# Norm sums apart from the last block, inverted blocks requested ahead of the set, and a semaphore for the rows alone, in a one-core diffusion block

## The chip, the cores and the metric

The kernel runs on one core of one Trainium2 chip. The core has five engines that run their own instruction streams and meet through semaphores: TensorE (PE, matrix products), VectorE (DVE), ScalarE (ACT), GpSimd (POOL) and SyncE (SP, which here issues most of the DMAs). The metric is the device time of one execution in microseconds (us), lower is better; of several runs the median counts.

## The reference, cut to what matters

One layer of a diffusion backbone works on 256 latent tokens and 256 context tokens with 2048 channels each. A half-step SwiGLU feed-forward net (FFN1) runs over both streams, then a token mixer, then a second feed-forward net (FFN2) over the latent stream only, then a last norm. Each part begins with a root-mean-square norm and a shift and scale.

```
def rmsnorm(x, g):
    y = xf * lax.rsqrt(jnp.mean(xf * xf, axis=-1, keepdims=True) + EPS)
    return (y * g.astype(jnp.float32)).astype(x.dtype)
...
def chunk_gated_delta(q, k, v, g, beta, s0):
    """Chunked gated delta rule S_t = a_t S_{t-1}(I - b_t k_t k_t^T) + b_t k_t v_t^T, o_t = S_t^T q_t."""
    n = L // CHUNK
...
    sol = lax.linalg.triangular_solve(eye + a_low, rhs, left_side=True, lower=True, unit_diagonal=True)
    u_val, w_kd = sol[..., :GDN_DV], sol[..., GDN_DV:]
    qk = jnp.einsum('nbhid,nbhjd->nbhij', qc, kc) * decay

    def step(S, xs):
        q_i, k_i, u_i, w_i, g_i, qk_i = xs
        v_new = u_i - jnp.einsum('bhck,bhkv->bhcv', w_i, S)
...
def mixer_out(p, o, z, w_pool, pool_scale, o_norm_g, w_out):
    y = jnp.concatenate([pool_mixer(p[..., :POOL_W], w_pool, pool_scale),
                         gdn_gate_out(o, z, o_norm_g)], axis=-1)
    return y @ w_out
...
    for li in range(DEPTH):
        h = h + 0.5 * ml[:, 2][:, None] * swiglu(
            modulate(rmsnorm(h, norm_g[li, 0]), ml[:, 0], ml[:, 1]), ffn_w_in[li, 0], ffn_w_out[li, 0])
...
        pl = modulate(rmsnorm(h, norm_g[li, 1]), ml[:, 3], ml[:, 4]) @ w_in[li]
...
        h = h + ml[:, 5][:, None] * mixer_out(pl, ol_f + ol_b, zl, w_pool[li], pool_scale[li],
                                              o_norm_g[li], w_out[li])
        h = h + 0.5 * ml[:, 8][:, None] * swiglu(
            modulate(rmsnorm(h, norm_g[li, 2]), ml[:, 6], ml[:, 7]), ffn_w_in[li, 1], ffn_w_out[li, 1])
    return rmsnorm(h, final_g)
```

The DeltaNet part has 8 heads, chunks of 64 tokens and two directions; each chunk needs the inverse of a unit lower triangular 64 by 64 matrix.

## The kernel before, in words

Every weight is used as two parts: ACT writes the rounded high part `wh` of a tile that SP loaded into `raw`, DVE the rest `wl = raw - wh` (a *split*, about 1.2 us), and PE makes three products with them (L698, L699, L700). This pair of splits runs some tiles ahead of PE, in the order in which the tiles are used, and so also in every gap of the other work of ACT and DVE.

The stages in time: norm 0 and the modulation vectors (to 110 us), FFN1 (11 groups, to 1588), norm 1, the projections and preparation of the 8 heads (1601 to 1941), the token tiles of the pooling part (to 1977), eight scans (`scan(h)`, 1977 to 2156), the output projection, norm 2 (2203 to 2210), FFN2, norm 3 (2965) and the output.

**Norms.** ACT squares the 16 blocks of 128 channels of the residual as they are finished, into `sq[:, 0]` and `sq[:, 1]` in turn. POOL adds 14 of them into `nacc`. PE's `norm(n, ...)` then waits for all squares and sums over partitions with 128 by 1 products: for each tile of 128 tokens one of `nacc`, one of `sq[:, 0]`, one of `sq[:, 1]`, into one column of a bank (12 products for 512 tokens, 6 for 256). DVE's `mean_square` makes `n_ms`, POOL raises it to -0.5 (`n_rstd`), PE spreads it over the partitions, DVE and ACT make the normalized blocks `xh` and `xl` (`x2h` and `x2l` in norm 2), and PE starts on the next weights. In `normed`, DVE runs `between(m)`, a split of a coming weight tile, after each second block.

**The inversion.** `lanes(b, part)` on POOL inverts 32 by 32 diagonal blocks of four heads at a time (batch `b` = heads 4b to 4b+3) by 31 steps of two instructions each, in three parts (`LANE_STEPS`), and at the end copies `XL` transposed to `XP`. SP's `lane_store(b)` writes both to HBM (`d_x`, `d_xp`, 512 KB each, semaphore `fg_out`). For each head, `level_load(h)` reads eight 32 KB pieces back into `CX` and `CP` (after `placed` of the head before) and 384 KB of rows `UF` (after `pe_y64` of the head before), all on one semaphore, `level_in`. POOL's `place(h)` waits for these nine, copies the pieces into block diagonal places of `GI` and `FI` (16 copies, L2220 and L2226) and raises `placed`. PE's `join_y32(h)` and what follows (*the join* of head h, from L1075 on) wait for `placed` and build the inverse of the 64 by 64 matrices. `scan(h)` runs the join of head h+1 between its own first products; the join of head 0 runs inside the token tiles. `out_power(h)` on POOL serves the output norm of head h after its scan.

**SP's order.** SP works its requests in program order and waits in place. In the loop over the scans it first stores (`lane_store(1)`, in turn h = 2), then `set_load(h + 1)` (six requests, 1.7 MB, after `pe_av` of the head before last), then `level_load(h + 2)`, then tiles of the output weight (`out_load`). The calls `FILL_AT` place pieces of the pooling part (`pool_linear`, `means`) between the steps of a scan.

Of the kernel before, what the change touches and what calls it, by code (L numbers as in the profile page):

```python
# [13 lines left out]
P = 128  # L14
# [112 lines left out]
LANE_STEPS = (((0, 11), (11, 21), (21, BLK - 1)), ((0, 13), (13, 23), (23, BLK - 1)))  # L127
SET_DMAS = 6
LEVEL_DMAS = 2 * NBLK + 1
# [5 lines left out]
FILL_AT = ((3, 5, 6), (0, 1, 2, 3, 5, 6), (0, 1, 2, 3, 5, 6)) + 5 * ((0, 2, 3, 5, 6),)  # L135
# [78 lines left out]
def build(nc, xT, ctxT, cols_in, ada_in_w, masks_in, pools_in, w_out_t, w_ada, w_in, a_log, dt_bias,  # L214
# [14 lines left out]
    with es:  # L229
# [164 lines left out]
        mk_in, ba_in, rowc_in = sem("mk_in"), sem("ba_in"), sem("rowc_in")  # L394
# [57 lines left out]
        def bc(ap, n):  # L452

            return ap.unsqueeze(1).broadcast_to([P, n, ap.shape[-1]])

# [14 lines left out]
        def _(sp):  # L470
# [137 lines left out]
            def level_load(h):  # L608
# [26 lines left out]
            for h in range(HEADS + 2):  # L635
                for k in range(K_TILES):
# [25 lines left out]
            lane_load(HEADS - 1)  # L662
# [3 lines left out]
            level_load(1)  # L666
# [26 lines left out]
        def _(pe):  # L693
# [267 lines left out]
            def decay_sums():  # L961
                pe.wait_ge(prep_dve, PREP_G)
                pe.wait_ge(mk_in, 16)
# [94 lines left out]
            def join_y32(h):  # L1058

                sl, bank = h % 2, JOIN_BANK(h)  # L1060
                pe.wait_ge(HS["placed"], at("placed", h, 1))
                if h >= 2:
# [170 lines left out]
            norm(1, NTOK, 7)  # L1233
# [28 lines left out]
            norm(2, SEQ, 4)  # L1262
            with pe.Fori(0, GROUPS) as g:
                group(1, g, 0, T_FFN2, x_base=2 * KT)
            norm(3, SEQ, 4)
# [3 lines left out]
        def _(act):  # L1269
# [19 lines left out]
            def square(n, k, streams):  # L1289
# [3 lines left out]
                for s in range(streams):  # L1293
                    i = fn(sq[:, k % 2, s * SEQ:(s + 1) * SEQ], (h_lat, h_ctx)[s][:, k, :], ACT.Square)  # L1294
# [33 lines left out]
            def group(f, r, s, base, width=0, closing=None, early=None, begun=0):  # L1328
                for j in range(GROUP_TILES):
                    if j >= begun:  # L1330
# [16 lines left out]
            def squares(n, f, streams, blocks):  # L1347

                for k in blocks:
                    act.wait_ge(gated[f], gates(f, 0, LAST if f < 2 else 1, 0) + (k + 1) * streams)  # L1350
                    square(n, k, streams)

            def decay_prep():
                act.wait_ge(prep_dve, 1)
                act.wait_ge(rowc_in, 32)
# [206 lines left out]
            with act.Fori(0, PIECE_ONE) as r:  # L1562
# [3 lines left out]
                  early=decay_weights)  # L1566
            for k in range(K_TILES):
                high(1, 2 * k)
                high(1, 2 * k + 1)
                split(0, 0, T_HEADS + k + AHEAD)  # L1570
            act.wait_ge(x_ready, 2 * KT)
            act.dma_start(rowc[:, 0, :], dt_bias.rearrange("l d h -> l (d h)").broadcast_to([P, 16])).then_inc(rowc_in, 16)
            act.dma_start(rowc[:, 1, :], a_log.rearrange("l d h -> l (d h)").broadcast_to([P, 16])).then_inc(rowc_in, 16)
# [746 lines left out]
```

## Time and profile before

| | |
|---|---|
| runs | 2977.45, 2975.01, 2976.6 us; median 2976.6 us |
| profiled execution | 2981.67 us, its span 2979.8 us, mean granted clock of TensorE 0.982 |
| PE busy | 2885.3 us, 97% of the span |
| DVE / ACT / POOL busy | 1682.2 (56%) / 963.8 (32%) / 235.3 us (8%) |
| DMA | 541.62 MB, mean 182 GB/s |

The span is that of the profiled execution from the first to the last instruction; the time of that execution is 1.9 us longer. A busy time is the time in which the engine executes; PE is busy nearly throughout, so its idle stretches and the stretches in which its granted clock is low are what there is to look at.

### The profile page before, as it was taken

The numbers are of one execution on the slowest core, as the hardware profiler recorded it, in microseconds if no ns is written. First come the engines' busy times: TensorE is split into PE (matmuls) and PEld (weight loads), VectorE is DVE, ScalarE is ACT, GpSimd is POOL, SyncE is SP. The second block draws the span as 40 slices with busy tenths as digits, with TensorE's granted clock in tenths as the row PEclk, the third lists the DMA queues.
The fourth block names the chain that finished last, engine by engine and source line by source line (L and its number), as shares of the span: only waits on it lengthen the run. The fifth ranks groups of instructions, "written<-read, shape, count | busy, mean of one in ns | idle before, by whom it ended". The sixth has DMA issues, their size and how long they took to land. (4 is left out here: it accounts for less than half of the span.)

```text
span 2979.8 us, 47716 instructions
## 1 busy us (share of the span) xinstructions
PE 2885.3 (97%) x18176; PEld 2523.8 (85%) x18176; DVE 1682.2 (56%) x2465; ACT 963.8 (32%) x1434; POOL 235.3 (8%) x390
## 2 busy tenths in 40 slices
PE   5999999999999999999998999988989999999998
PEld 3677888888888888888887888868889999999998
DVE  2522557566575747566536666735565555555555
ACT  2212222222122222122124555533344443443443
POOL 3000000000000000000001113463120000000001
PEclk8999999999999999999999999989999999999999
DMA  9764255545455766757423566675555566565564
GB/s 361 285 211 159 92 155 156 164 147 169 140 174 171 247 198 224 230 192 259 142 85 88 152 191 189 197 226 153 158 155 181 185 186 187 181 187 183 183 190 133
DMA packets 399049, 541.62 MB, mean 182 GB/s; under 512 B 51024, under 2 KB 301904, under 8 KB 390240
## 3 DMA queue, kind: packets, MB, share of 16 engines
q1 hardware_dynamic: 377264, 434.20, 46.9%
q10 hardware_dynamic: 21680, 106.03, 11.0%
q8 instruction: 65, 1.06, 0.1%
q14 instruction: 40, 0.33, 0.0%
HBM read 518.08 MB, written 22.05 MB: 181 GB/s over the span
## 5 line engine op out<-in xcount | busy, mean ns | idle before, releaser
L1626 DVE TENSOR_TENSOR wl<-raw,wh 128x1024 fp32r<-128x1024 f32 x640 | 782.4, 1232 | 775.2 <-ACT wh L1278 773.5
L1278 ACT CAST wh<-raw 128x1024 fp32r<-128x1024 f32 x640 | 666.1, 1047 | 1548.1 <-PE ps L700 1177.4
L698 PE MATMUL ps<-xh,wh 128*128 128x512 f32 (+1 forms) x1920 | 733.7, 382 | 7.1 <-issue 4.6
L699 PE MATMUL ps<-xl,wh 128*128 128x512 f32 (+1 forms) x1920 | 724.3, 377 | 0.0
L700 PE MATMUL ps<-xh,wl 128*128 128x512 f32 (+1 forms) x1920 | 723.3, 377 | 0.0
L698 PE MATMUL ps<-hth,wh 128*128 128x512 f32 (+1 forms) x1408 | 471.3, 335 | 0.6 <-DVE wl L1626 0.6
L699 PE MATMUL ps<-htl,wh 128*128 128x512 f32 (+1 forms) x1408 | 470.3, 334 | 0.0
L700 PE MATMUL ps<-hth,wl 128*128 128x512 f32 (+1 forms) x1408 | 470.3, 334 | 0.0
L698 PEld LDWEIGHTS ps<-xh,wh 128*128 128x128 f32 x1920 | 363.5, 189 | 78.2 <-issue 9.4
L700 PEld LDWEIGHTS ps<-xh,wl 128*128 128x128 f32 x1920 | 362.8, 189 | 68.1
L699 PEld LDWEIGHTS ps<-xl,wh 128*128 128x128 f32 x1920 | 363.4, 189 | 64.7
L698 PE MATMUL ps<-x2h,wh 128*128 128x256 f32 x1408 | 395.6, 281 | 6.4 <-DVE x2l L1682 6.3
L699 PE MATMUL ps<-x2l,wh 128*128 128x256 f32 x1408 | 393.5, 279 | 0.0
L700 PE MATMUL ps<-x2h,wl 128*128 128x256 f32 x1408 | 393.4, 279 | 0.0
L1723 DVE SCALAR_TENSOR_TENSOR acc<-abuf,cT,acc 128x1024 f32<-128x1024 f32 x240 | 297.0, 1279 | 0.0
L698 PEld LDWEIGHTS ps<-hth,wh 128*128 128x128 f32 x1408 | 264.3, 188 | 29.2 <-DVE wl L1626 1.0
L700 PEld LDWEIGHTS ps<-hth,wl 128*128 128x128 f32 x1408 | 264.5, 188 | 27.5
L699 PEld LDWEIGHTS ps<-htl,wh 128*128 128x128 f32 x1408 | 263.8, 187 | 27.1
L698 PEld LDWEIGHTS ps<-x2h,wh 128*128 128x128 f32 x1408 | 265.0, 188 | 7.8 <-issue 7.7
L700 PEld LDWEIGHTS ps<-x2h,wl 128*128 128x128 f32 x1408 | 265.4, 188 | 0.0
L699 PEld LDWEIGHTS ps<-x2l,wh 128*128 128x128 f32 x1408 | 264.0, 188 | 0.0
L2183 POOL TENSOR_TENSOR nacc<-hf 128x512 f32<-128x512 f32 (+1 forms) x4 | 4.4, 1108 | 2250.7 <-ACT hf L1294 2250.7
(245 smaller groups left out, 2342.7 us busy)
## 6 DMA issues: line engine op xcount, KB each, us to landing
raw<-in_ffn_w_in SPq DMA_DIRECT2D x704, 256.0 KB, 3.2
raw<-in_ffn_w_out SPq DMA_DIRECT2D x176, 512.0 KB, 4.2
abuf<-in_w_ada ACTq DMA_DIRECT2D x64, 1024.0 KB, 6.0
ada_t<-in_ada SPq DMA_DIRECT2D x64, 512.0 KB, 9.1
abuf<-in_w_ada ACTq DMA_DIRECT2D x64, 512.0 KB, 3.7
raw<-in_w_in SPq DMA_DIRECT2D x128, 256.0 KB, 3.4
gate_t<-in_ada SPq DMA_DIRECT2D x32, 512.0 KB, 4.9
raw<-in_w_out SPq DMA_DIRECT2D x32, 512.0 KB, 4.3
```

Of the source, the lines that this page charges most:

```text
L698: mm(out, ah, bh, start=first, stop=False)
L699: mm(out, ah, bl, start=False, stop=False)
L700: return mm(out, al, bh, start=False, stop=last)
L1278: nc.scalar.copy(wh[:, t % HL, :], raw[:, t % RAW, :]).then_inc(hi_done, 1)
L1626: tt(wl[:, t % HL, :], raw[:, t % RAW, :], wh[:, t % HL, :].bitcast(F32), ALU.subtract).then_inc(lo_done, 1)
L1723: n = stt(acc[:, b, :], src, c_, acc[:, b, :], ALU.mult, ALU.add)
L2183: i = tt(nacc[:, 0:nt], sq[:, 0, 0:nt], sq[:, 1, 0:nt], ALU.add)
```

## The change

(a) `norm(n)`: PE sums `nacc` and `sq[:, 0]` as soon as 15 of the 16 blocks are squared, and the squares of the last block apart, into a bank of their own (`LAST_BANK`). DVE makes `n_ms` from the first sums and adds the last block's in a second instruction (`stt`); POOL waits for both. ACT's squares of a block wait for each stream apart.

(b) `normed`: in norm 1 one split is left out of the last FFN1 group (`left=1`) and done as the first `between`; in norm 2 the first `between` is empty; each of the others stands one place later and one at the end.

(c) SP: `level_load` becomes `level_blocks` (the eight pieces) and `level_rows` (`UF`, with a semaphore `rows_in` that PE's join waits for and POOL no longer). `lane_store(0)` is some tiles earlier, and so are the blocks and rows of head 0; `level_blocks(1)` is ahead of `set_load(0)`; in the loop over the scans `level_blocks(h + 2)` is ahead of `set_load(h + 1)`, except in turns 0 and 2; in turn 2 `set_load(3)` is ahead of `lane_store(1)`.

(d) POOL: `place(1)` follows `place(0)` at once; `lanes(1, part)` are one turn later against the places, and the second batch's parts are steps 0 to 12, 13 to 25 and 26 to 30 (before 13 to 22 and 23 to 30).

(e) The second scan has its fillers at other steps. (f) `mk_in` and `rowc_in` become one semaphore.

```diff
-LANE_STEPS = (((0, 11), (11, 21), (21, BLK - 1)), ((0, 13), (13, 23), (23, BLK - 1)))
+LANE_STEPS = (((0, 11), (11, 21), (21, BLK - 1)), ((0, 13), (13, 26), (26, BLK - 1)))
...
-FILL_AT = ((3, 5, 6), (0, 1, 2, 3, 5, 6), (0, 1, 2, 3, 5, 6)) + 5 * ((0, 2, 3, 5, 6),)
+FILL_AT = ((3, 5, 6), (0, 2, 3, 4, 5, 6), (0, 1, 2, 3, 5, 6)) + 5 * ((0, 2, 3, 5, 6),)
...
-            def level_load(h):
+            def level_blocks(h):
...
+            def level_rows(h):
+
                 if h:
                     sp.wait_ge(HS["pe_y64"], at("pe_y64", h - 1, 1))
                 sp.dma_start(UF[0:3 * BLK].rearrange("p m c -> p (m c)"),
-                             d_uf[h, 0:3 * BLK].rearrange("p m c -> p (m c)")).then_inc(HS["level_in"], 16)
+                             d_uf[h, 0:3 * BLK].rearrange("p m c -> p (m c)")).then_inc(rows_in, 16)
...
+                    if h == HEADS and k == K_TILES - 2:
+                        lane_store(0)
                     if h == HEADS + 1 and k == 0:
-                        lane_store(0)
+                        level_blocks(0)
+                        level_rows(0)
...
-                    if h == HEADS + 1 and k == 3:
-                        level_load(0)
...
+            level_blocks(1)
             lane_load(HEADS - 1)
             set_load(0)
             out_load(0)
             out_load(1)
-            level_load(1)
+            level_rows(1)
...
             for h in range(HEADS):
+
+                last = h in (0, 2)
+                if h + 2 < HEADS and not last:
+                    level_blocks(h + 2)
+                if h + 1 < HEADS:
+                    set_load(h + 1)
                 if h == 2:
                     lane_store(1)
-                if h + 1 < HEADS:
-                    set_load(h + 1)
                 if h + 2 < HEADS:
-                    level_load(h + 2)
+                    if last:
+                        level_blocks(h + 2)
+                    level_rows(h + 2)
...
             def norm(n, nt, bank):
 
+
                 pe.wait_ge(nacc_done, (KT - 3) * (n + 1))
-                pe.wait_ge(sq_done, KT * (n + 1))
+                pe.wait_ge(sq_done, KT * (n + 1) - 1)
                 for t in range(nt // P):
                     x_ = slice(t * P, (t + 1) * P)
                     mm(ps[:, bank, t:t + 1], nacc[:, x_], ones, start=True, stop=False)
-                    mm(ps[:, bank, t:t + 1], sq[:, 0, x_], ones, start=False, stop=False)
-                    i = mm(ps[:, bank, t:t + 1], sq[:, 1, x_], ones, start=False, stop=True)
+                    i = mm(ps[:, bank, t:t + 1], sq[:, 0, x_], ones, start=False, stop=True)
+                i.then_inc(stat_pe, 1)
+                pe.wait_ge(sq_done, KT * (n + 1))
+                for t in range(nt // P):
+                    i = mm(ps[:, LAST_BANK[n], t:t + 1], sq[:, 1, t * P:(t + 1) * P], ones, start=True, stop=True)
                 i.then_inc(stat_pe, 1)
...
             def squares(n, f, streams, blocks):
 
+                last = gates(f, 0, LAST if f < 2 else 1, 0)
                 for k in blocks:
-                    act.wait_ge(gated[f], gates(f, 0, LAST if f < 2 else 1, 0) + (k + 1) * streams)
-                    square(n, k, streams)
+                    square(n, k, streams, lambda s: act.wait_ge(gated[f], last + k * streams + s + 1))
...
+                dve.wait_ge(stat_pe, 2 * n + 2)
+                stt(m, ps[:, LAST_BANK[n], 0:nt // P], 1.0 / D, m, ALU.mult, ALU.add).then_inc(ms_done, 1)
...
                 low(n, KT - 1)
                 between(KT // 2 - 1)
+                between(KT // 2)
...
-            normed(2, SEQ, 4, lambda k: split(0, 0, T_FFN2 + k + AHEAD))
+            normed(2, SEQ, 5, lambda m: split(0, 0, T_FFN2 + m + AHEAD - 1) if m else None)
...
             place(0)
+            place(1)
             lanes(1, 0)
-            for h in range(HEADS):
+            for h in range(1, HEADS):
                 if h + 1 < HEADS:
                     place(h + 1)
-                if h:
-                    out_power(h - 1)
-                if h + 1 < len(LANE_STEPS[1]):
-                    lanes(1, h + 1)
+                out_power(h - 1)
+                if h < len(LANE_STEPS[1]):
+                    lanes(1, h)
             out_power(HEADS - 1)
```

How the instructions stand at three places of two engines:

POOL before, from the last copy of `place(0)` on: the zeroing of `XL` and then 13 inversion steps of the second batch, the last of which is the sixth row, ahead of the first copy of `place(1)`.

```order
L2226 COPY FI<-CX 32x4x32
L2240 MEMSET XL 128x1024 [waits fg_out,lt_in,gdn_placed]
L2242 MEMSET XL 128x32 [waits xl_zero]
L2249 TENSOR_TENSOR tm<-LT,XL 128x31 [waits xl_zero]
...
L2254 TENSOR_TENSOR XL<-XL,tm 128x19x13 [waits lane_step]
L2220 COPY GI<-CX 32x4x32 [waits gdn_pe_tn64,gdn_level_in,lane_step]
```

POOL of the change at the same place:

```order
L2255 COPY FI<-CX 32x4x32
L2249 COPY GI<-CX 32x4x32 [waits gdn_pe_tn64,gdn_level_in,gdn_placed]
...
L2255 COPY FI<-CX 32x4x32
L2269 MEMSET XL 128x1024 [waits fg_out,lt_in,gdn_placed]
L2271 MEMSET XL 128x32 [waits xl_zero]
L2278 TENSOR_TENSOR tm<-LT,XL 128x31 [waits xl_zero]
```

`place(1)` has moved ahead of the first part of the inversion of the second batch.

POOL before, from the last copy of `place(2)` to `place(3)`: `out_power(0)`, then the third part of the second batch to its end and `XP`.

```order
L2226 COPY FI<-CX 32x4x32
L2192 TENSOR_TENSOR ors<-oms,mhalf 128x2 [waits gdn_oms_set,gdn_placed]
L2249 TENSOR_TENSOR tm<-LT,XL 128x192 [waits lane_step,gdn_ors_set]
...
L2254 TENSOR_TENSOR XL<-XL,tm 128x31 [waits lane_step]
L2257 COPY XP<-XL 128x1024 [waits lane_step]
L2220 COPY GI<-CX 32x4x32 [waits gdn_pe_tn64,gdn_level_in,lanes_done]
```

POOL of the change, from the end of the second part to `place(4)`: `place(3)` and `out_power(1)` now stand ahead of the third part.

```order
L2283 TENSOR_TENSOR XL<-XL,tm 128x6x26 [waits lane_step]
L2249 COPY GI<-CX 32x4x32 [waits gdn_pe_tn64,gdn_level_in,lane_step]
...
L2255 COPY FI<-CX 32x4x32
L2221 TENSOR_TENSOR ors<-oms,mhalf 128x2 [waits gdn_oms_set,gdn_placed]
L2278 TENSOR_TENSOR tm<-LT,XL 128x135 [waits lane_step,gdn_ors_set]
L2283 TENSOR_TENSOR XL<-XL,tm 128x5x27 [waits lane_step]
...
L2286 COPY XP<-XL 128x1024 [waits lane_step]
L2249 COPY GI<-CX 32x4x32 [waits gdn_pe_tn64,gdn_level_in,lanes_done]
```

The end of the inversion of heads 4 to 7 has moved behind the output norm of the second scan.

SP before, in turn 2 of the loop over the scans: the store of the second batch (`d_x`, `d_xp`), then the set of head 3 (`s_khT` to `s_z`), then the pieces of head 4.

```order
L633 DMA raw<-in_w_out 128x1024 [waits lo_done]
L590 DMA d_x<-XL 128x1024 [waits lanes_done]
L590 DMA d_xp<-XP 128x1024
L604 DMA s_khT<-d_khT 128x512 [waits gdn_pe_av,gdn_y_set]
...
L606 DMA s_z<-d_z 128x256
L616 DMA CX<-d_x 32x8x32 [waits gdn_placed,fg_out]
```

SP of the change in the same turn:

```order
L639 DMA raw<-in_w_out 128x1024 [waits lo_done]
L607 DMA s_khT<-d_khT 128x512 [waits gdn_pe_av,gdn_y_set]
...
L609 DMA s_z<-d_z 128x256
L593 DMA d_x<-XL 128x1024 [waits lanes_done]
L593 DMA d_xp<-XP 128x1024
L619 DMA CX<-d_x 32x8x32 [waits gdn_placed,fg_out]
```

The store stands right ahead of the reading of what it stored, behind the set.

## Rows read from the trace of the kernel before

**Rows 1.** What PE waits for: releaser, us in all, count, longest.

```profile
PE ps L1075 <- POOL FI L2226: 18.7, 6, 8.6
PE ps L732 <- POOL n_rstd L2189: 11.2, 4, 7.8
PE ps L698 <- DVE x2l L1682: 6.3, 4, 2.7
PE ps L1211 <- DVE yl L2069: 3.8, 2, 2.0
```

**Rows 2.** Timeline at norm 1: start, us, engine, line, operation [idle before <- releaser].

```profile
1589.30 0.40 ACT L1294 ACTIVATE hf<-h_ctx 128x256 f32<-128x256 f32 x1
1589.85 0.35 PE L726 MATMUL ps<-cols,nacc 128*128 128x1 f32 x2 [1.81 <-ACT hf L1294]
1593.08 0.16 DVE L1660 TENSOR_SCALAR n_ms<-ps 128x4 f32<-128x4 f32 x1 [1.18 <-PE ps L728]
1594.40 2.07 PE L732 MATMUL ps<-cols,n_rstd 128*128 128x128 f32 x8 [1.35 <-POOL n_rstd L2189]
```

**Rows 3.** Windows by stage: stretch, us; PE, PEld, DVE, ACT, POOL busy; PEclk; DMA; GB/s.

```profile
1954.00:1977.00 23.00, 22.56 (x183) 17.80 (x184) 7.40 (x9) 7.79 (x13) 11.63 (x21) 0.85 0.95 302
1977.00:2009.80 32.80, 22.40 (x207) 19.69 (x207) 8.64 (x26) 9.35 (x29) 27.66 (x62) 0.74 0.57 189
2009.80:2038.00 28.20, 23.94 (x227) 20.93 (x226) 12.50 (x37) 9.36 (x27) 13.14 (x34) 0.88 0.30 85
2038.00:2057.60 19.60, 19.00 (x245) 18.04 (x244) 13.08 (x37) 8.77 (x26) 3.53 (x9) 1.00 0.89 257
2057.60:2077.60 20.00, 17.61 (x233) 16.58 (x232) 11.59 (x34) 8.29 (x28) 4.81 (x18) 1.00 0.63 196
2077.60:2141.50 63.90, 58.60 (x692) 55.41 (x691) 37.51 (x102) 23.54 (x69) 13.77 (x45) 0.89 0.53 160
```

**Rows 4.** PE's timeline where the joins of heads 0, 1 and 4 begin.

```profile
1954.44 0.37 PE L1075 MATMUL ps<-GI,UF 32*32 32x32 f32 x6 [3.89 <-POOL FI L2226]
...
1988.73 0.26 PE L1075 MATMUL ps<-GI,UF 32*32 32x32 f32 x2 [8.63 <-POOL FI L2226]
...
2060.16 0.22 PE L1075 MATMUL ps<-GI,UF 32*32 32x32 f32 x2 [1.96 <-POOL FI L2226]
```

**Rows 5.** POOL's timeline from the token tiles to the scan of head 2.

```profile
1949.01 0.28 POOL L2220 COPY GI<-CX 32x128 f32<-32x128 f32 x1 [14.85 <-DMA UF<-d_uf]
...
1951.83 1.19 POOL L2226 COPY FI<-CP 32x128 f32<-32x128 f32 x1
...
1984.20 0.28 POOL L2220 COPY GI<-CX 32x128 f32<-32x128 f32 x1
...
2013.91 0.41 POOL L2249 TENSOR_TENSOR tm<-LT,XL 128x135 f32<-128x135 f32 x1
...
2018.08 1.98 POOL L2257 COPY XP<-XL 128x1024 f32<-128x1024 f32 x1
...
2039.33 0.69 POOL L2192 TENSOR_TENSOR ors<-oms,mhalf 128x2 f32<-128x2 f32 x1 [2.60 <-DVE oms L1969]
...
2054.64 0.28 POOL L2220 COPY GI<-CX 32x128 f32<-32x128 f32 x1 [14.61 <-DMA UF<-d_uf]
```

**Rows 6.** DVE's timeline: a split in the token tiles, and one in norm 2.

```profile
1951.60 1.26 DVE L1626 TENSOR_TENSOR wl<-raw,wh 128x1024 fp32r<-128x1024 f32 x1 [3.19 <-ACT wh L1278]
...
2215.82 1.23 DVE L1626 TENSOR_TENSOR wl<-raw,wh 128x1024 fp32r<-128x1024 f32 x1 [3.07 <-ACT wh L1278]
```

**Rows 7.** SP's queue in the scan of head 2: issue start, us, line, transfer.

```profile
2042.38 0.32 SPq L604 DMA_DIRECT2D s_khT<-d_khT  x1
...
2045.63 0.45 SPq L606 DMA_DIRECT2D s_z<-d_z  x1
```

**Rows 8.** DMA issues of 2037 to 2056 and 1986 to 2000: KB each, median us to landing.

```profile
d_xp<-XP SPq DMA_DIRECT2D x1, 512.0 KB, 6.0
...
CX<-d_x SPq DMA_DIRECT2D x4, 32.0 KB, 2.0
```

More of the change, by code:

```diff
@@ L393, in build @@
             sem("fin_done"), sem("fin_pool"), sem("fin_scaled"), sem("rb_set"), sem("out_done"))
-        mk_in, ba_in, rowc_in = sem("mk_in"), sem("ba_in"), sem("rowc_in")
+        ba_in, prep_in, rows_in = sem("ba_in"), sem("prep_in"), sem("rows_in")
         ba_hi, ba_split, ba_done, prep_dve, prep_act, prep_pe = (
@@ L962, in decay_sums @@
                 pe.wait_ge(prep_dve, PREP_G)
-                pe.wait_ge(mk_in, 16)
+                pe.wait_ge(prep_in, 48)
                 for q in range(4):
@@ L1061, in join_y32 @@
                 pe.wait_ge(HS["placed"], at("placed", h, 1))
+                pe.wait_ge(rows_in, 16 * (h + 1))
                 if h >= 2:
@@ L1232, in _ @@
                 group(0, r, 3, 3 * GROUP_TILES, reduced=True)
-            norm(1, NTOK, 7)
+            norm(1, NTOK, 6)
             pe.wait_ge(ba_split, 1)
@@ L1261, in _ @@
                 out_heads(d, range(HEADS))
-            norm(2, SEQ, 4)
+            norm(2, SEQ, 5)
             with pe.Fori(0, GROUPS) as g:
                 group(1, g, 0, T_FFN2, x_base=2 * KT)
-            norm(3, SEQ, 4)
+            norm(3, SEQ, 5)
         @block.scalar
@@ L1287, in start, with square @@
                 fn(cT[:], cols[:, C_C:C_C + 2 * KT], ACT.Silu).then_inc(c_silu, 1)
-            def square(n, k, streams):
+            def square(n, k, streams, final=None):
                 if k >= 2:
@@ L1293, in square @@
                 for s in range(streams):
+                    if final is not None:
+                        final(s)
                     i = fn(sq[:, k % 2, s * SEQ:(s + 1) * SEQ], (h_lat, h_ctx)[s][:, k, :], ACT.Square)
@@ L1565, in _ @@
             group(0, 0, LAST, LAST * GROUP_TILES, closing=lambda b: squares(1, 0, 2, range(4 * b, 4 * b + 4)),
-                  early=decay_weights)
+                  early=decay_weights, left=1)
             for k in range(K_TILES):
@@ L1569, in _ @@
                 high(1, 2 * k + 1)
-                split(0, 0, T_HEADS + k + AHEAD)
+                split(0, 0, T_HEADS + k + AHEAD - 1)
+            split(0, 0, T_HEADS + K_TILES + AHEAD - 1)
             act.wait_ge(x_ready, 2 * KT)
-            act.dma_start(rowc[:, 0, :], dt_bias.rearrange("l d h -> l (d h)").broadcast_to([P, 16])).then_inc(rowc_in, 16)
-            act.dma_start(rowc[:, 1, :], a_log.rearrange("l d h -> l (d h)").broadcast_to([P, 16])).then_inc(rowc_in, 16)
-            act.dma_start(mk[:], masks_in.rearrange("p (m n) -> p m n", n=P)).then_inc(mk_in, 16)
+            act.dma_start(rowc[:, 0, :], dt_bias.rearrange("l d h -> l (d h)").broadcast_to([P, 16])).then_inc(prep_in, 16)
+            act.dma_start(rowc[:, 1, :], a_log.rearrange("l d h -> l (d h)").broadcast_to([P, 16])).then_inc(prep_in, 16)
+            act.dma_start(mk[:], masks_in.rearrange("p (m n) -> p m n", n=P)).then_inc(prep_in, 16)
             for h in range(HEADS):
@@ L1605, in _ @@
                 high(2, 2 * k + 1)
-                split(0, 0, T_FFN2 + k + AHEAD)
+                if k:
+                    split(0, 0, T_FFN2 + k + AHEAD - 1)
+            split(0, 0, T_FFN2 + K_TILES + AHEAD - 1)
             group(1, 0, 0, T_FFN2, begun=K_TILES)
@@ L1658, in mean_square @@
             def mean_square(n, nt, bank):
[L1659 to L1660 removed]
+                m = n_ms[:, 0:nt // P]
+                dve.wait_ge(stat_pe, 2 * n + 1)
+                ts(m, ps[:, bank, 0:nt // P], 1.0 / D, EPS, ALU.mult, ALU.add).then_inc(ms_done, 1)
+                dve.wait_ge(ms_done, 2 * n + 1)
+                dve.wait_ge(stat_pe, 2 * n + 2)
+                stt(m, ps[:, LAST_BANK[n], 0:nt // P], 1.0 / D, m, ALU.mult, ALU.add).then_inc(ms_done, 1)
             SCALE = ((0, 1), (2, 3), (4,))
@@ L1771, in decay_weights, with group @@
                 tt(wbal[:], wba[:], wbah[:].bitcast(F32), ALU.subtract).then_inc(ba_split, 1)
-            def group(f, r, s, base, evac=False, width=0, then=None, late=None, begun=0):
+            def group(f, r, s, base, evac=False, width=0, then=None, late=None, begun=0, left=0):
                 for j in range(GROUP_TILES):
-                    if j >= begun:
+                    if begun <= j < GROUP_TILES - left:
                         split(r, GROUP_TILES, base + j + AHEAD)
@@ L1804, in decay_prep @@
                 dve.wait_ge(ba_done, 2)
-                dve.wait_ge(rowc_in, 32)
+                dve.wait_ge(prep_in, 48)
                 link(tt(xg, ba[:, :, 16:32], bc(rowc[:, 0, :], 4), ALU.add))
@@ L2131, in _ @@
                 group(0, r, 7, 7 * GROUP_TILES, evac=True, width=2)
-            group(0, 0, LAST, LAST * GROUP_TILES, evac=True, then=modulations, late=decay_weights)
-            normed(1, NTOK, 7, lambda k: split(0, 0, T_HEADS + k + AHEAD))
+            group(0, 0, LAST, LAST * GROUP_TILES, evac=True, then=modulations, late=decay_weights, left=1)
+            normed(1, NTOK, 6, lambda m: split(0, 0, T_HEADS + m + AHEAD - 1))
             dve.wait_ge(x_ready, 2 * KT)
```

17 lines of the change are left out of this document (8 added, 9 removed).

## Prediction

> **What bounds the kernel now.** I read the page first: PE is busy for 97% of the span, and the chain that ended last is nearly all PE. A change that doesn't touch PE's products can therefore win only PE's idle time, and the time that a low clock adds to its work. So the second view is what PE waits for [rows 1]. The join of a head waited for POOL's copies six times, 18.7 us in all; the norms waited 11.2 us for `n_rstd` (7.8 of it in norm 0), 6.3 us for DVE's low parts in norm 2, and 3.8 us twice for the pooling part `yl`. These four lines are 40 us, and the change aims at all four. The third view is the windows by stage [rows 3], for the granted clock: the scan of head 0, which holds the longest wait, has 0.74; that of head 2, where no join waits, and that of head 3, with one wait of 1.96, have 1.00; the three after them, 0.89 together. A low clock here means 1.2 instead of 2.4 GHz for part of the stretch. An unstalled scan is read from the row of 2057.60: 20.00 us less its wait of 1.96 [rows 4] leaves 18.04 us at clock 1.00.
>
> The profiled execution took 2981.67 us, 5.1 us above the median of the runs, 2976.6. I sum the terms against the former and carry the difference over to the median.
>
> **The norms.** In norm 1 the last square ends at 1589.70 [rows 2], PE starts its 12 sums at 1589.85, and DVE has `n_ms` at 1593.08: 3.4 us for twelve sums. With the change eight of them run before the last square is there and four stay behind it. Two thirds of the 3.2 us from the first sum to `n_ms` are 2.1; I take 2.0. ACT's squares no longer wait for both streams, which I put at one square's 0.4, so **2.4** (2.0 to 2.8). The new second instruction of DVE replaces one of 0.16 us on the path, so it costs nothing there; the first one is done early, hidden by the last square. In norms 2 and 3 six sums become two behind the last square, half of norm 1's: **0.9** each. In norm 0 there is one DVE instruction more and DVE is the late engine: **-0.2**. In norm 2 a split on DVE waited 3.07 us for ACT's high part [rows 6], and the low parts of the blocks queued behind it; PE waited for them four times, 6.3 us, the longest (2.7) for the first block, which stays. The other three, 3.6 us, go if the split stands one place later: by then PE has used the tile whose place ACT's high part waits for, and two more blocks' low parts stand ahead of it in DVE's queue. So norm 2 is 0.9 + 3.6 = **4.5** (0.9 to 4.5).
>
> **Token tiles and the join of head 0.** PE waited 3.89 us [rows 4]. `place(0)` started at 1949.01, released by the rows `UF` [rows 5], which the copies don't use. With `rows_in` apart and the requests earlier in SP's queue it can start earlier; I take 2.5 us, since the pieces themselves still cost eight requests and their landing, and `place(0)` also waits for the last spills of `q` and `z`. The stage has a clock of 0.85 over 23.00 us [rows 3], which is 3.45 us missing. I take 2.9 of it back, so **5.4**; ends: 2.5 (the wait alone) and 7.3 (3.89 + 3.45).
>
> One copy in `place(0)`, 1951.83, took 1.19 us where its like take 0.28, while DVE's split of 1951.60 to 1952.86 ran [rows 5, 6]. The Trainium skill (SBUF — State Buffer, "Who interferes with whom") says that a DVE instruction with two SBUF inputs contends with a GpSimd instruction that reads SBUF, and the split is one; the row agrees. It speaks against part (d): the last inversion steps move from a stretch of POOL without splits into the scan of head 2, where DVE splits. By the rule that part would cost one such excess, 0.9, more, and the sum would be 30.7 instead of the 31.6 below; I go by the measured duration without it.
>
> **Scan of head 0.** `place(1)` started at 1984.20 [rows 5], only after 13 inversion steps, and PE waited 8.63 for it [rows 4]. With the change it stands right behind `place(0)`, waits only for the join of head 0 to release `GI`, and takes some 4.5 us (1984.20 to 1988.73): it is done near 1969, and PE wants it near 1975 to 1980. The wait goes: 8.6. The clock missing in this scan is 0.26 x 32.80 = 8.5 us; none of it on work would give 8.6, two fifths of it 12.0. I take the middle, **10.3**. The first part of the second batch now runs behind `place(1)`, under the first scan, where nothing waits for it.
>
> **Scan of head 1.** 28.20 us at clock 0.88 [rows 3], with the two waits for `yl` of 3.8 us in all [rows 1] and 0.12 x 28.20 = 3.4 us of missing clock, 7.2 together. The new places of the fillers give DVE one step more between `pool_linear` parts; I expect one of the two waits to go (1.8), the other to shorten to 1.5, and most of the clock to come back: **5.0** (2.0 to 7.2).
>
> **Scan of head 2** has no wait and full clock, so **0**.
>
> **Scan of head 3: the price.** This is where the stall goes. In the kernel before, the second batch was inverted by 2020.06 (`XP` 2018.08 + 1.98), long before the scan of head 2 began at 2038.0. Now its last five steps and `XP` stand behind `out_power(1)`, which ended at 2040.0 (2039.33 + 0.69) [rows 5]. These steps and the copy took 2013.91 to 2020.06 = 6.15 us, so they end 8.2 us into that scan, at 2046.2 in the old times. The store stands behind the set of head 3, which SP issued from 2042.38 to 2046.1 [rows 7], so the queue costs nothing more: set and inversion end together. Store: 0.9 us to issue two, and 6.0 to land [rows 8], gives 2053. Then eight requests at 0.45 us each and 2.0 to land [rows 8], 5.7, gives 2058.8, and `place(4)`, 5.5 us in this place (2054.64 to 2060.16) [rows 4, 5], 2064.3. PE wanted it at 2058.2 (2060.16 less 1.96). Queueing in the DMAs moves this by a us or so either way; I take a stall of 5.5 where 1.96 was, -3.5. The last three scans lose 1.9 us of clock each with waits of 1 to 2 us (below); for this longer one I take 2.5: **-6.0** together. Ends: -11 if the store waits a further 5 us, and +2 if the chain is done in time.
>
> **Scans of heads 4 to 6.** 63.90 us [rows 3]; three unstalled ones are 3 x 18.04 = 54.1, so 9.8 can be won. Their three waits for POOL are 18.7 - 3.89 - 8.63 - 1.96 = 4.2 us [rows 1, 4]; the rest, 5.6, is clock, 1.9 a scan. `place` now starts on the pieces alone: `place(4)` of before was released by `UF` [rows 5], as were these. Since `level_blocks` stand ahead of the set, they are requested as soon as the previous head is placed, and the copies end before PE comes: **9.3**, from 4.2 (clock not regained) to 9.8.
>
> **Edits at nothing.** The merged semaphore `prep_in`: three transfers that land long before their use. The earlier `lane_store(0)` and pieces of head 0: they push the weight tiles behind them in SP's queue by ten requests of 0.45 us, 4.5 us, covered by the tiles that are loaded ahead; without that cover PE would lose up to those 4.5 us once. `set_load(h + 1)`, now behind eight requests of 0.45 us (3.6 us) that wait for `placed(h + 1)`: it waited for `pe_av` some 4.4 us into the scan anyway (2042.38 against 2038.0), and lands well before the next scan wants it.
>
> **Sum.** -0.2 + 2.4 + 5.4 + 10.3 + 5.0 + 0 - 6.0 + 9.3 + 4.5 + 0.9 = 31.6. The profiled execution would be at 2950.1, the median at 2976.6 - 31.6 = 2945. All low ends together give 9.9 (2967), all high ones 46.7 (2930).
>
> **The rivals.** *B, no new wait at head 4*: the store lands faster than 6.0 and the pieces are read in under 5.7 us, so that the -6.0 becomes 0 to +2: 2938. For it: the queue is less loaded than when the row was taken. Against: four dependent steps in series, each from a row. *C, only the waits go*: the clock doesn't come back since other short waits remain on PE, or POOL, whose order is now two places and then inversion, is late in the scan of head 1. Then the terms are 2.5 + 8.6 + 2.0 + 4.2 for the scans, -6 for head 4, 5.9 for the norms less part of norm 2: about 17, 2960. For it: three waits of 4.2 us together went with 5.6 us of missing clock. *D, nothing moves*: the waits are replaced by others of the same length, as when the pieces arrive late because all eight stand ahead of sets and rows: 2976. Against: the 8.63 are in POOL's order alone, and that is changed. *E, slower*: `set_load(h + 1)` is stuck behind `level_blocks(h + 2)`, which waits for `placed(h + 1)` while SP stands. If the place of the next head is done only 12 us or more after a scan's start, the set lands too late and the next scan begins late; the excess would be some 9 us in each of the four scans where this order applies, 37 us, against the 31.6 won: 2982. It decides from placing about 11 us into the scan; the row of before has 2.5 us (2060.1 against 2057.6) and the new order aims lower.
>
> **Chances.** My sum 0.55, B 0.15, C 0.22, D 0.04, E 0.04. Runs of this kernel can't tell changes under about 0.2%, 6 us, from none. Faster by more: 0.92; within: 0.04; slower: 0.04. The range goes from 2932 (most of B) to 2964 (most of C); D and E and the tails of the others stay out. The predicted time is that of my sum, 2945.
>
> **What would show it.** In the changed profile the wait of PE at the first product of the join should be under 2 us for head 0, gone for heads 1, 2, 3, 5, 6 and 7, and 4 to 7 us for head 4, with the store of the second batch issued some 8 us into the scan of head 2. PE's clock should be near 1.00 in the scans of heads 0, 1, 4, 5 and 6 and lower in that of head 3. Between the last square and `n_ms` of norm 1 there should be about 1.4 us, and in norm 2 one wait for a low part where four were. I am wrong if the clock stays low without long waits (C), if the chain of the second batch is shorter than its four steps (B), or if a set lands after its scan wants it (E).

## The result and the profile after

The changed kernel took 2953.82 us (median of 7 runs, 2928.54 to 2957.31) where before took 2977.85 (7 runs, 2975.01 to 2980.98): the ratio is 0.9921, 95% interval 0.9891 to 0.995. That is 24.0 us faster; 31.6 had been forecast, and the time lies inside the range of 2932 to 2964. One of the seven executions of the change came some 25 us earlier than the rest, as did four of twelve of x10 below and three of 19 of before in the comparison of x9 and x10; gains here are differences of medians, from which the ratios of x9 and x10 therefore stand apart, and nothing here shows why some come early.

The profiled execution of the change took 2957.31 us with a span of 2955.5 (before 2979.8). What PE waited for, to be read beside [rows 1]:

```profile
PE ps L750 <- POOL n_rstd L2218: 9.0, 4, 5.3
PE ps L1094 <- POOL FI L2255: 6.2, 2, 5.1
PE ps L1200 <- ACT vn L1522: 3.8, 1, 3.8
PE ps L712 <- DVE x2l L1710: 2.7, 1, 2.7
PE ps L1063 <- DVE AY L1954: 2.3, 1, 2.3
PE ps L1230 <- ACT u L1558: 1.6, 1, 1.6
```

The six waits for POOL's copies are two, and of 18.7 us 6.2 are left. The waits for `x2l` went from four to one, and the two waits for `yl` of the pooling part became one for `u` at the same product. Two lines are new: 3.8 us for `vn` (the new values of a scan's step, `v_new` in the reference, which ACT copies out of PE's banks), and 2.3 us for `AY` (a matrix that DVE makes in the preparation of a head). The windows of the same stages as in [rows 3] (token tiles, then the scans of heads 0, 1, 2, 3 and 4 to 6; the columns are those of rows 3):

```profile
1948.00:1971.20 23.20, 22.91 (x197) 17.86 (x195) 7.95 (x10) 8.21 (x14) 10.14 (x30) 1.00 0.97 287
1971.20:1998.70 27.50, 23.19 (x204) 20.36 (x205) 10.33 (x28) 9.93 (x30) 17.43 (x38) 0.75 0.77 253
1998.70:2021.10 22.40, 20.42 (x227) 18.45 (x227) 12.58 (x37) 9.39 (x27) 20.09 (x38) 1.00 0.34 105
2021.10:2043.10 22.00, 20.54 (x244) 19.51 (x243) 13.49 (x36) 8.81 (x25) 8.63 (x18) 0.92 0.51 160
2043.10:2069.00 25.90, 20.54 (x232) 19.43 (x232) 11.67 (x34) 8.25 (x28) 9.13 (x33) 0.80 0.68 211
2069.00:2122.90 53.90, 52.66 (x692) 49.75 (x691) 36.94 (x102) 23.60 (x69) 11.51 (x35) 1.00 0.63 190
```

The last row is the plainest: three scans in 53.90 us at clock 1.00, 17.97 each, where 63.90 at 0.89 stood. The row above it is the price: the scan of head 3 takes 25.90 at 0.80, where it took 20.00 at 1.00. The scan of head 0 got shorter, but its clock (0.75) hasn't recovered.

At norm 1, ACT, DVE and PE of the change, to be read beside [rows 2]:

```profile
1588.95 0.42 ACT L1315 ACTIVATE hf<-h_ctx 128x256 f32<-128x256 f32 x1
...
1590.69 0.16 DVE L1688 SCALAR_TENSOR_TENSOR n_ms<-ps,n_ms 128x4 f32<-128x4 f32 x1 [0.81 <-PE ps L746]
...
1592.01 2.08 PE L750 MATMUL ps<-cols,n_rstd 128*128 128x128 f32 x8 [1.43 <-POOL n_rstd L2218]
```

From the end of the last square to `n_ms` are 1.3 us (1589.37 to 1590.69) where 3.4 were; 1.4 had been forecast.

For the balance I took the starts and ends of the same PE instructions in both traces (the scans from the first product of `vn` and `s_kd`, a part of the head's set, in one to that in the next) and set the differences beside the terms of the prediction. us gained:

| stage | forecast | measured |
|---|---|---|
| norm 0, modulation, FFN1 | -0.2 | 0.0 (1523.21 to 1523.18) |
| norm 1, last product of FFN1 to first of the heads | 2.4 | 2.4 (13.01 to 10.65) |
| heads' projections up to the join of head 0 | 0 | -2.7 (349.50 to 352.17) |
| token tiles and the join of head 0 | 5.4 | 6.1 (3.89 to 0, 22.85 to 20.71) |
| scan of head 0, with its start | 10.3 | 5.2 (2.10 to 4.48, 30.41 to 22.80) |
| scan of head 1 | 5.0 | 5.8 (28.23 to 22.38) |
| scan of head 2 | 0 | -2.4 (19.57 to 22.02) |
| scan of head 3 | -6.0 | -5.9 (19.99 to 25.89) |
| scans of heads 4 to 6 | 9.3 | 10.0 (63.92 to 53.91) |
| norm 2 and the blocks behind it | 4.5 | 5.0 (7.43 to 6.53, 754.16 to 750.07) |
| norm 3 | 0.9 | 0.8 (4.84 to 4.05) |
| sum | 31.6 | 24.3 |

One pair of executions doesn't resolve every row of this table. Up to the end of FFN1 all the kernels below run what the change runs; in their profiles FFN1 ended between 1584.5 and 1588.3 us, and norm 1 took 9.7 to 10.7. In the scans of heads 2 and 3, x10 has the same instructions in the same order as the change:

```profile
2018.78:2039.26 20.48, 19.04 (x245) 18.01 (x243) 14.44 (x36) 8.84 (x26) 8.48 (x18) 1.00 0.52 167
2039.26:2067.15 27.89, 20.54 (x232) 19.43 (x231) 11.68 (x34) 8.26 (x28) 9.12 (x33) 0.82 0.65 200
```

There the two took 20.48 and 27.89 us, in the change 22.02 and 25.89: nearly the same together, 1.5 and 2.0 us apart by themselves, with waits of 1.01 and 7.13 us where the change has 1.04 and 5.14.

### The profile page after: what moved, and what is told of

Its sections match the earlier page's. It is cut to its first block and busy times, and to the rows that moved or that the text cites. A ratio compares the mean times of both kernels' runs of the same rounds, so it can differ in the third digit from the quotient of the medians.

```text
span 2955.5 us, 47731 instructions
## 1 busy us (share of the span) xinstructions
PE 2880.7 (97%) x18176; PEld 2521.3 (85%) x18176; DVE 1683.2 (57%) x2469; ACT 963.9 (33%) x1434; POOL 235.9 (8%) x390
```

## The experiments

Unless said otherwise each kernel is the change with one edit. All were timed beside the kernel before, whose medians were 2977.4 to 2978.9 us; the gains below are against those. Executions of one kernel commonly lie 3 to 12 us apart, so where a time differs from the change's by less than some 6 us, the profile has to tell the two apart.

**The end of the second batch** (x3; the term of -6.0). The edit:

```diff
-LANE_STEPS = (((0, 11), (11, 21), (21, BLK - 1)), ((0, 13), (13, 26), (26, BLK - 1)))
+LANE_STEPS = (((0, 11), (11, 21), (21, BLK - 1)), ((0, 18), (18, BLK - 1)))
...
+                if h == 2:
+                    lane_store(1)
                 if h + 1 < HEADS:
                     set_load(h + 1)
-                if h == 2:
-                    lane_store(1)
```

> The change, but the second batch is inverted in two parts, steps 0 to 17 and 18 to 30 with the copy XP, so that it ends ahead of the copies of head 3, and SP stores it ahead of the set of head 3. Theory (the wait of 5.14 us at head 4 and the half clock behind it are the price of the late end of the batch): store about 10 us earlier, no wait at head 4, the scan of head 3 at 18 instead of 25.9 us: 7.9 us faster than the change, about 2946. Rival (18 steps are too long for POOL ahead of the copies of head 2, and the wait only moves to heads 2 and 3): waits of 3 us or more there, 2952 to 2956.

Measured: 2945.32 us, ratio 0.9885 (0.987 to 0.99), a gain of 33.6, which is 9.5 beyond the change. First the chain in the profile of the change, from POOL's, SP's and PE's timelines; these are the links of the forecast:

```profile
2028.69 2.06 POOL L2286 COPY XP<-XL 128x1024 f32<-128x1024 f32 x1
...
2044.33 0.28 POOL L2249 COPY GI<-CX 32x128 f32<-32x128 f32 x1 [13.59 <-DMA CP<-d_xp]
```

```profile
2029.10 0.43 SPq L609 DMA_DIRECT2D s_z<-d_z  x1
2030.77 0.32 SPq L593 DMA_DIRECT2D d_x<-XL  x1
2031.13 0.43 SPq L593 DMA_DIRECT2D d_xp<-XP  x1
2038.48 0.32 SPq L619 DMA_DIRECT2D CX<-d_x  x1
```

```profile
2048.90 0.32 PE L1094 MATMUL ps<-GI,UF 32*32 32x32 f32 x4 [5.14 <-POOL FI L2255]
```

The inversion ends at 2030.75 (9.6 us into the scan; 8.2 forecast), SP stores at once, reads back 7.7 us later when the store has landed, POOL copies from 2044.33, and PE waits 5.14 us. In the experiment the same links, from POOL and SP:

```profile
2013.30 1.97 POOL L2286 COPY XP<-XL 128x1024 f32<-128x1024 f32 x1
2015.33 0.28 POOL L2249 COPY GI<-CX 32x128 f32<-32x128 f32 x1
...
2035.11 0.28 POOL L2249 COPY GI<-CX 32x128 f32<-32x128 f32 x1 [12.76 <-DMA CP<-d_xp]
```

```profile
2020.53 0.43 SPq L593 DMA_DIRECT2D d_x<-XL  x1
...
2028.51 0.38 SPq L619 DMA_DIRECT2D CX<-d_x  x1
```

`XP` is there 15 us earlier, the store is issued 10 us earlier, and the copies 9. PE's list of waits has no row for `FI` above 0.9 us; the scans of heads 2 and 3 take 19.59 and 17.97 where the change has 22.02 and 25.89. The theory holds: the wait at head 4 was the late end of the batch. The wait at head 3 (1.04 us in the change) went too: steps 18 to 30 took 14.6 us, steps 13 to 25 in the change 17.9, so that even with `XP` (2.0) ahead of it `place(3)` starts at 2015.33, in the change at 2017.21. The rival's waits at heads 2 and 3 didn't come.

**POOL's order at head 1** (x2; the wait of 8.6). `lanes(1, 0)` and `place(1)` change places:

```diff
             place(0)
-            place(1)
             lanes(1, 0)
+            place(1)
```

> The change, but POOL does the first part of the second batch's inversion ahead of the copies of head 1, as before. Theory (the 8.6 us wait of head 1 came from POOL's order alone): the inversion part runs about 1961 to 1979, the copies end near 1983.5, PE waits some 6.5 us for them and loses 2 us of clock: 8.5 us slower than the change, about 2962. Rival (requesting the pieces ahead of the set did it): no wait at head 1, 2954.

Measured: 2964.67 us, ratio 0.9953 (0.994 to 0.9967); 14.2 us won, 9.8 less than by the change. On PE:

```profile
1980.45 0.27 PE L1094 MATMUL ps<-GI,UF 32*32 32x32 f32 x2 [9.38 <-POOL FI L2255]
```

The wait is back, 3 us longer than I had worked out, in spite of the pieces requested early. POOL's order made it.

**The new wait for `vn`** (x6; the forecast did not have it). In the change, ACT at the start of the first scan:

```profile
1973.58 1.04 ACT L1297 CAST wh<-raw 128x1024 fp32r<-128x1024 f32 x1 [1.75 <-DMA raw<-in_w_out]
1974.65 1.07 ACT L1615 COPY u<-ps 128x512 f32<-128x512 f32 x2
1975.61 0.45 ACT L1522 COPY vn<-ps 128x128 f32<-128x128 f32 x2
```

`vn` stands in ACT's queue behind the high part of the third tile of the output weight, and that waited for the tile to land. PE came there 5.7 us earlier than before (1972.18 instead of 1977.89), the tile landed only 3.4 us earlier (1973.56 instead of 1977.00), since the set, two tiles and `UF` are ahead of it. The edit puts it ahead:

```diff
             lane_load(HEADS - 1)
-            set_load(0)
             out_load(0)
             out_load(1)
-            level_rows(1)
             out_load(2)
+            set_load(0)
+            level_rows(1)
             out_load(3)
```

> The change, but SP requests the first three tiles of the output weight ahead of the set of head 0. Theory (the new wait of 3.77 us for ACT's vn at the start of the first scan comes from the third of these tiles, whose landing ACT's queue waits for ahead of vn): it lands 5 us sooner, the wait falls to about 1.5 us as before, and the half clock of the 13 us after it mostly goes: 4 us faster, about 2950. Rival (vn waits for its own chain): wait unchanged, 2954; or the set lands too late and PE waits for it, 2956.

Measured: 2947.20 us, ratio 0.9903 (0.9888 to 0.9918), 6.8 us beyond the change. The first two scans in windows:

```profile
1966.50:1987.10 20.60, 18.46 (x204) 16.14 (x205) 7.28 (x25) 7.59 (x27) 16.04 (x40) 1.00 0.95 300
1987.10:2011.20 24.10, 22.12 (x228) 19.71 (x228) 12.81 (x37) 9.38 (x27) 21.70 (x43) 0.93 0.36 107
```

The wait is gone (a new one of 0.84 us for the set, which lands later, stands ahead of that scan), the first scan has clock 1.00 instead of 0.75 and takes 20.60 instead of 27.50. Measured between the same products, its start went from 4.48 to 0.81 us and its length from 22.80 to 19.74: the wait of 3.8 us had cost 6.7 with the low clock (1.2 GHz in part of the stretch) that went with it. The next three scans together give 0.6 of it back. That of head 1 takes 24.05 (22.38) at clock 0.93, with no wait for POOL; why its clock fell isn't shown. That of head 2 takes 19.60 (22.02) without the wait for POOL. That of head 3 takes 27.23 (25.89): POOL's inversion doesn't get faster, PE comes to the join of head 4 earlier and waits 7.48 us for it.

**The semaphore or the order, heads 5 to 7.** One kernel (x4) keeps the order and makes `place` wait for the rows again; the other (x5) keeps the semaphore and puts the pieces behind the set:

```diff
                 pool.wait_ge(HS["level_in"], at("level_in", h, PER["level_in"]))
+                pool.wait_ge(rows_in, 16 * (h + 1))
```

> The change, but POOL's copies of each head also wait for the rows, as before (SP's order stays the new one). Theory as the prediction put it (the copies of heads 5 to 7 win because they start on the pieces alone): their waits of 1 to 2 us and the lost clock are back, 9 us, with some more at heads 1 and 4: about 2966 to 2970. Rival (the order of the requests alone frees heads 5 to 7, since the copies wait for the scan's vn products anyway, 2 us behind the pieces): no wait at heads 5 to 7; only heads 1 to 4 shift, because the rows of head 1 land 10 us behind its pieces and hold back the inversion: waits at heads 2, 3 and 4 grow by 1, 3 and 5 us, about 2963.

```diff
-                last = h in (0, 2)
+                last = True
```

> The change, but SP requests the pieces of head h + 2 behind the set of head h + 1 in every turn of the loop over the scans, as before; the copies still don't wait for the rows. Theory (heads 5 to 7 need one of the two, the order or the semaphore, not both: behind the set the pieces land about 13.3 us into a scan, the copies end at 17.8, and PE comes at 18.6): no wait at heads 5 to 7, 2954 as the change. Rival (the prediction's reason: they win because the pieces stand ahead of the set): waits of 1 to 2 us and lost clock in three scans, about 2960 to 2963.

Measured: 2965.00 (0.9952, 0.9939 to 0.9966) and 2959.22 (0.9942, 0.9929 to 0.9956). PE's waits for POOL in the first, with the rows of heads 4 and 6 and POOL's start of `place(4)`, then those of heads 6 and 7 in the second:

```profile
PE ps L1094 <- POOL FI L2256: 15.8, 7, 9.3
...
2051.96 0.26 PE L1094 MATMUL ps<-GI,UF 32*32 32x32 f32 x2 [9.31 <-POOL FI L2256]
...
2092.78 0.22 PE L1094 MATMUL ps<-GI,UF 32*32 32x32 f32 x2 [2.71 <-POOL FI L2256]
...
2047.43 0.28 POOL L2250 COPY GI<-CX 32x128 f32<-32x128 f32 x1 [16.39 <-DMA UF<-d_uf]
```

```profile
2081.06 0.22 PE L1094 MATMUL ps<-GI,UF 32*32 32x32 f32 x2 [1.36 <-POOL FI L2255]
2100.13 0.25 PE L1094 MATMUL ps<-GI,UF 32*32 32x32 f32 x4 [1.03 <-POOL FI L2255]
```

Neither theory holds whole. The scans of heads 4 to 6 took 58.9 us with the order alone (18.20, 22.25, 18.40) and 56.6 with the semaphore alone (18.17, 19.39, 19.07); with neither 63.9, with both 53.9. In time either part wins half or more, and their gains overlap (5.0 and 7.3, together 10.0). In waits it is otherwise: of 4.2 us with neither, 3.2 are left with the order alone and 2.5 with the semaphore alone, and only both together remove them. Most of what one part wins alone is clock: five of these six scans have 1.00, that with the wait of 2.71 us 0.92, where before had 0.85, 0.92 and 0.92. By time alone x5 can't be told from the change; its profile is of its fastest execution (2951.73).

About half of what it costs to wait for the rows is elsewhere, but not for the reason that the rival gave. At head 1 a wait of 1.43 us came back (the scan of head 0 takes 24.95 instead of 22.80), and the wait at head 4 grew from 5.14 to 9.31. `place(1)` does start only when the rows have landed (1971.04 instead of 1962.69), but POOL waits for DVE at `out_power(0)` in both kernels and has made up for it there (1998.96, in the change 1998.47): `XP` is done 9.5 us into the scan of head 2, in the change 9.6, and the waits at heads 2 and 3 didn't grow. What is late is `place(4)` itself: its pieces had landed at 2045.00, its rows only at 2047.23, and that is 2.2 us of the 4.2; another 1.6 come from PE, which is there earlier because the scan of head 2 took 20.45 us and not 22.02.

**The norms alone** (x1). The kernel before with parts (a), (b) and (f); SP's and POOL's orders and the fillers of before.

> Only parts (a), (b) and (f) of the change; SP's and POOL's orders, the parts of the inversion and the fillers are those of before, and the copies of a place wait for the rows too, as before. Theory (the norm terms of the prediction are each a gain of their own): 2.4 + 4.5 + 0.9 - 0.2 = 7.6 us, so about 2970 where before has 2977.8; first product of norm 1 some 2.4 us earlier, in norm 2 one wait for a low part instead of four. Rival (what norm 1 wins is waited for again in the heads' projections, where the profile of the change shows a wait of 2.25 us for AY that before had not): 5 us, about 2973, with that wait in this profile too.

Measured: 2969.15 us, ratio 0.9969 (0.9957 to 0.998), 9.7 us won (the interval, 6 to 13 us, holds the 7.6 of the theory and the rival's 5 lies just outside). In the profile norm 1 takes 10.64 us, norm 2 6.53 and the blocks behind it 749.54, as in the change. The wait for `AY` is in it too, so it can't come from SP's or POOL's order:

```profile
PE ps L1059 <- DVE AY L1950: 1.8, 1, 1.8
```

It is not the norms' either: five of the other kernels (x2, x4, x5, x6 and x7) have the same instructions up to there and no such wait, and their heads take 349.5 to 349.8 us.

**The split of norm 2 at its old place** (x10), in ACT's program and in DVE's:

```diff
-                if k:
-                    split(0, 0, T_FFN2 + k + AHEAD - 1)
-            split(0, 0, T_FFN2 + K_TILES + AHEAD - 1)
+                split(0, 0, T_FFN2 + k + AHEAD)
...
-            normed(2, SEQ, 5, lambda m: split(0, 0, T_FFN2 + m + AHEAD - 1) if m else None)
+            normed(2, SEQ, 5, lambda m: split(0, 0, T_FFN2 + m + AHEAD) if m < K_TILES else None)
```

> The change, but in norm 2 the splits stand at the places of before. Theory (three of the four waits of norm 2 come from the split that stands one place too early in DVE's queue): the waits of 1.40, 1.11 and 1.10 us are back, 3.6 us slower, about 2957. Rival (the norm's apart sums removed them, since all of it is earlier by 0.9 us): one wait only, 2954.

Measured: 2956.47 us, ratio 0.9918 (0.9882 to 0.9953), which alone doesn't tell it from the change. The profile does:

```profile
PE ps L712 <- DVE x2l L1708: 6.3, 4, 2.7
```

The four waits are those of [rows 1], and the blocks behind norm 2 take 755.12 us where the change has 750.07. The split's place made them; the apart sums didn't remove them.

**The fillers of the second scan as before** (x8):

```diff
-FILL_AT = ((3, 5, 6), (0, 2, 3, 4, 5, 6), (0, 1, 2, 3, 5, 6)) + 5 * ((0, 2, 3, 5, 6),)
+FILL_AT = ((3, 5, 6), (0, 1, 2, 3, 5, 6), (0, 1, 2, 3, 5, 6)) + 5 * ((0, 2, 3, 5, 6),)
```

> The change, but the fillers of the second scan at the steps of before. Theory (the fillers were worth one of the two waits for the pooling part): two waits of 2.0 and 1.8 us where the change has one of 1.55, and half clock behind them: 3 to 5 us slower, 2957 to 2959. Rival (that scan is faster for the clock alone, because the first scan no longer ends late): one wait, 2954.

Measured: 2958.85 us, ratio 0.9933 (0.992 to 0.9947), 4.9 less won than by the change; here too the profile has to tell:

```profile
PE ps L1230 <- DVE yl L2098: 3.8, 2, 2.0
PE ps L1094 <- POOL FI L2255: 8.5, 2, 7.0
```

Both waits for `yl` are back and that scan takes 26.57 us instead of 22.38; the next takes 19.72 instead of 22.02, since POOL then has the time for its 13 steps ahead of `place(3)`, and the one after 27.71. The filler's places are worth 4.2 us in their scan, some of it passed on.

**Both remedies together** (x7), the earlier end of the batch (18 and 13 steps) and the tiles ahead of the set:

> The change with the second batch ended sooner and the first three output tiles ahead of the set of head 0. Theory (the two are independent): the gains of both add, 8.5 and 4 us, about 2941. Rival (the first scan's wait only moves the same work): 2945.

Measured: 2946.75 us, ratio 0.9902 (0.9887 to 0.9917). They don't add: 31.2 us won, 7.2 beyond the change, where 9.5 and 6.8 would be 16.3. With the first scan shorter, 18 steps are too many ahead of `place(2)`:

```profile
1993.35 0.24 PE L1094 MATMUL ps<-GI,UF 32*32 32x32 f32 x3 [3.44 <-POOL FI L2255]
```

The scan of head 1 takes 30.69 us. **Cut otherwise** (x9), into 15 and 16 steps:

```diff
-LANE_STEPS = (((0, 11), (11, 21), (21, BLK - 1)), ((0, 18), (18, BLK - 1)))
+LANE_STEPS = (((0, 11), (11, 21), (21, BLK - 1)), ((0, 15), (15, BLK - 1)))
```

> The change with the first three output tiles ahead of the set of head 0, and the second batch in two parts of 15 and 16 steps (before its store ahead of the set of head 3). Theory (with the first scan shorter, POOL's inversion sets the pace; 18 steps ahead of the copies of head 2 were too long by 3.4 us, and 13 left POOL idle for 2.4 us, room for two steps): no wait above 2 us at heads 2, 3 and 4, scans of 20, 23, 20.5 and 18 us, about 2939 where the two edits with 18 steps gave 2947. Rival (POOL has too much to do for the shorter scans whichever way it is cut): a wait of 3 us or more at head 3 or 4, 2945.

Measured: 2945.06 us, ratio 0.9907 (0.9875 to 0.9939). The wait at head 2 is gone, the one at head 3 is 3.21 us (scans of 20.12, 24.01, 23.80 and 17.95):

```profile
PE ps L1094 <- POOL FI L2255: 4.6, 2, 3.2
```

That is the rival's case. POOL has the same work in a shorter time, and with the tiles ahead of the set one join waited in each of the three cuts that were run: head 4 with 13, 13 and 5 steps (7.48 us, x6), head 2 with 18 and 13 (3.44, x7), head 3 with 15 and 16 (3.21, x9). The kernels x3, x9, x7 and x6 are 33.6, 32.4, 31.2 and 30.8 us under before; their intervals overlap, so which of them is fastest isn't shown.

## Why the prediction was right, point by point

- **The direction and the larger part of the sum** came as forecast: 24.0 of 31.6 us, about half way between the sum and the 17 of rival C. Of the waits that the change aims at the long ones of heads 0 and 1, three of four in norm 2 and those of heads 5 to 7 are gone, and the clock came back in the token tiles and in the scans of heads 1 and 4 to 6 (1.00). There rival C (only the waits go) is wrong; in the scan of head 0 (0.75) what it said came true, and the sign that the prediction named for that scan failed. B fell by the wait of 5.14 us at head 4; D and E fell by the time.
- **The price at head 4** was forecast by four links in series as a wait of 5.5 us and -6.0; measured 5.14 and -5.9, and shown by moving its cause (x3). That the numbers meet so closely is luck in part. Against the forecast the inversion ended 1.4 us later in the scan, the store took 0.8 longer and `place(4)` 0.9 less; and PE came 2.4 us later, since the scan of head 2 had become that much longer, which the forecast didn't have. In x10, where that scan took 20.48 us, the same chain made a wait of 7.13, and the scan of head 3 lost 7.9 where 6.0 had been forecast.
- **One of these links is a size**: the steps and `XP` took 2023.57 to 2030.75, 7.2 us instead of 6.15. One step took 1.10 us beside a split on DVE, 0.24 before without one:

```profile
2027.19 1.10 POOL L2278 TENSOR_TENSOR tm<-LT,XL 128x31 f32<-128x31 f32 x1
...
2026.91 1.29 DVE L1650 TENSOR_TENSOR wl<-raw,wh 128x1024 fp32r<-128x1024 f32 x1 [0.54 <-ACT wh L1297]
```

The rule that the prediction set beside the row (the Trainium skill, SBUF — State Buffer, "Who interferes with whom") would have put it 0.9 higher, and that is nearly the 1.0 measured. I went by the row without splits; for this link the rule would have been nearer. But the 5.5 us that the prediction took for `place(4)` had such a meeting in them too, and the 4.6 us of the change had none, so that over both links the two cancel. From the trace of before:

```profile
2055.43 1.28 POOL L2220 COPY GI<-CP 32x128 f32<-32x128 f32 x1
...
2055.29 1.27 DVE L1626 TENSOR_TENSOR wl<-raw,wh 128x1024 fp32r<-128x1024 f32 x1 [2.25 <-ACT wh L1278]
```

- **The scan of head 0 is the term that was mis-sized**: 10.3 forecast, 5.2 measured. The 8.6 us of POOL's order went, as forecast (x2). But the prediction asked only for what the join waits. PE came earlier to `vn` by more than the weight tile in ACT's queue ahead of it, so a wait of 1.5 us there grew to 3.8, and the scan kept a clock of 0.75. x6, which asks for that tile and the two before it ahead of the set, gave 6.8 us back.
- **The scan of head 2** was forecast at 0 and lost 2.4: ten steps of the inversion ahead of `place(3)` became thirteen, and I had moved the parts in the sum without their size. That made the wait of 1.04 us at head 3, where the prediction's own sign was none; it is gone in x3 and x8, with scans of 19.59 and 19.72. The rest is clock (0.92) and is not tied to that wait: x4, x5 and x10 have the wait (0.99 to 1.02), a clock of 1.00 and scans of 20.45 to 20.49.
- **The heads' projections** lost 2.7 us in this profile with a wait for `AY`. The change doesn't touch that stage; other profiles with the same instructions there have it or don't. What decides it stays open, and it is no part of the change.
- **Heads 5 to 7**: the size was right (9.3; 10.0), the reason half right. The prediction put it to the pieces alone and to their order; in time either half wins half or more alone, but only both together remove the waits (x4, x5).
- **The norms**: 2.4, 0.9 and 0.8 where 2.4, 0.9 and 0.9 were forecast; the split's place (3.6 forecast, 4.1 in the balance) is shown by x10.
- **Two slips in the prediction's sums** change little: eight requests of 0.45 us and 2.0 to land make 5.6 us, not 5.7, and all high ends together give 46.3, not 46.7, which is still 2930.

## What to carry to other kernels

When an engine is freed from one wait, look through each queue that it meets next for what doesn't come earlier by as much: here a weight tile that lands only 3.4 us earlier took half of the gain of its scan, and the wait for it cost 1.8 times its length, since the clock fell with it. When work of an off-path engine is moved behind something, follow it through every later step up to the one that waits (inversion, store, read, copy, join); here such a sum from single rows came out within half a microsecond, but only because links that were off by 0.8 to 2.4 us made up for each other. And when two remedies lean on the same engine, don't add their gains: its work has to fit into the shorter time.

## What the runs showed of the hardware

A short idle stretch of PE can cost more than its length: the wait of 3.77 us for `vn` went with a granted clock of 0.75 over 27.50 us, and without it the same scan had 1.00; the wait and its clock cost 6.7 us. It need not: the wait of 1.96 us at head 4 before [rows 4] went with 1.00 [rows 3], and the wait of 1.0 us at head 3 with 0.92 in the change and with 1.00 in x10.

A POOL instruction of 0.24 to 0.28 us that met a split on DVE took 1.10, 1.19 and 1.28 us, until the split was about done.

And the same two edits that win 9.5 and 6.8 us alone win 7.2 together (31.2 against 24.0): one engine off the critical path has to do the work of both in a shorter time, and a join waits 3.44 us for it that waited in neither alone.
